# A two-layer SSD/conformer/short-convolution block on one core: opening reordered, last output pair computed stream by stream, C of the last layer for latent tokens only, output turned inside the last stage

## The reference

```
for i in range(DEPTH):
    last = i == DEPTH - 1
    mx = (silu(c) @ w_mod[i] + b_mod[i]) ...      # nine modulation rows, latent
    mc = (silu(c_ctx) @ w_mod[i] + b_mod[i]) ...  # the same, context
    x = swiglu_half(x, mx, 0, ...)
    ctx = swiglu_half(ctx, mc, 0, ...)
    uc = modulate(ctx, norm_pre[i, 1], mc[3], mc[4])
    if last:    # of the context only the final scan states are used
        xs, Bm, Cm, dt, A = ssd_inputs(uc @ w_in[i][:, :SSD_IN], ...)
        s_f = ssd_final_state(xs, dt[:, :, 0], A[0], Bm)
        s_b = ssd_final_state(flip_seq(xs), ..., flip_seq(Bm))
    else:
        yc, s_f, s_b = mixer(uc @ w_in[i], ...)
        ctx = gated_residual(ctx, yc @ w_out[i], ...)
        ctx = swiglu_half(ctx, mc, 2, ...)
    ux = modulate(x, norm_pre[i, 1], mx[3], mx[4])
    yx, _, _ = mixer(ux @ w_in[i], s_f, s_b, ...)
    x = gated_residual(x, yx @ w_out[i], ...)
    x = swiglu_half(x, mx, 2, ...)
```

## Time and profile before

| | us |
|---|---|
| median of 3 runs (2392.0 to 2395.12) | 2392.99 |
| the profiled execution | 2389.37 |
| its span, first to last instruction | 2387.3 |
| PE busy, share of the span | 94% |
| DVE, ACT, POOL busy | 52%, 41%, 9% |
| mean granted TensorE clock, share of full speed | 0.969 |

### The profile page before, as it was taken

One profiled execution on the slowest core, in us unless ns is written; L12 is line 12 of the kernel. 1 busy time (PEld: TensorE's weight loads), 2 busy tenths in 40 slices (PEclk: granted clock), 3 DMA queues, 4 the chain that ended last, 5 costly groups with the idle time before them and its releaser, 6 DMA issues. The chain is left out here.

```text
span 2387.3 us, 28755 instructions
## 1 busy us (share of the span) xinstructions
PE 2238.6 (94%) x11753; PEld 1902.1 (80%) x11753; DVE 1241.7 (52%) x1759; ACT 984.9 (41%) x1477; POOL 224.0 (9%) x139
## 2 busy tenths in 40 slices
PE   5999999998988989999999999999999988889998
PEld 5788888876676768788888778888888776779998
DVE  4544453347769743544444445333324578855554
ACT  5444443244465343434443343222323444454443
POOL 0000000023322300100000000000001332300000
PEclk8999999999999989899999998999998999989999
DMA  6455454312332213255454441323332233334553
GB/s 219 142 171 164 159 167 159 97 56 71 90 124 87 73 53 101 76 172 163 159 169 162 150 137 56 103 90 105 119 97 69 71 107 97 107 117 131 187 179 122
DMA packets 282544, 291.05 MB, mean 122 GB/s; under 512 B 8286, under 2 KB 275502, under 8 KB 282414
## 3 DMA queue, kind: packets, MB, share of 16 engines
q1 hardware_dynamic: 281619, 287.04, 37.4%
q10 hardware_dynamic: 795, 2.18, 0.3%
HBM read 288.02 MB, written 1.18 MB: 121 GB/s over the span
## 5 line engine op out<-in xcount | busy, mean ns | idle before, releaser
L85 ACT ACTIVATE split<-raw 128x1024 fp32r<-128x1024 f32 (+1 forms) x368 | 382.8, 1040 | 938.2 <-PE bank L133 927.6
L93 DVE TENSOR_TENSOR split<-raw,split 128x1024 fp32r<-128x1024 f32 (+1 forms) x304 | 364.8, 1200 | 715.3 <-ACT split L85 715.3
L131 PE MATMUL bank<-uh,split 128*128 128x512 f32 (+1 forms) x1344 | 488.6, 364 | 1.1 <-DVE split L93 1.1
L133 PE MATMUL bank<-uh,split 128*128 128x512 f32 (+1 forms) x1344 | 488.3, 363 | 0.0
L132 PE MATMUL bank<-ul,split 128*128 128x512 f32 (+1 forms) x1344 | 488.3, 363 | 0.0
L133 PEld LDWEIGHTS bank<-uh,split 128*128 128x128 f32 x1344 | 253.9, 189 | 40.2
L131 PEld LDWEIGHTS bank<-uh,split 128*128 128x128 f32 x1344 | 254.1, 189 | 38.6 <-issue 1.5
L132 PEld LDWEIGHTS bank<-ul,split 128*128 128x128 f32 x1344 | 254.1, 189 | 36.5
L131 PE MATMUL bank<-hh,split 128*128 128x512 f32 (+1 forms) x704 | 256.6, 364 | 0.9 <-DVE split L93 0.9
L131 PE MATMUL bank<-mix_uh,split 128*128 128x512 f32 (+1 forms) x608 | 231.9, 381 | 27.2 <-POOL split L100 16.4
L133 PE MATMUL bank<-hh,split 128*128 128x512 f32 (+1 forms) x704 | 255.7, 363 | 0.0
(11 more groups left out here) (225 smaller groups left out, 2974.8 us busy)
## 6 DMA issues: line engine op xcount, KB each, us to landing
raw_mod<-in_w_mod SPq DMA_DIRECT2D x64, 1024.0 KB, 4.8
raw<-in_ffn_w_gate SPq DMA_DIRECT2D x44, 1024.0 KB, 5.1
raw<-in_ffn_w_up SPq DMA_DIRECT2D x44, 1024.0 KB, 5.1
raw<-in_w_in SPq DMA_DIRECT2D x40, 1024.0 KB, 5.1
raw<-in_ffn_w_down SPq DMA_DIRECT2D x32, 1024.0 KB, 4.9
raw<-in_w_out SPq DMA_DIRECT2D x16, 1024.0 KB, 4.9
raw<-in_ffn_w_down SPq DMA_DIRECT2D x16, 768.0 KB, 4.3
decay<-cum_rows SPq DMA_DIRECT2D x48, 256.0 KB, 3.4
```

The source lines that it names most:

```text
L85: ins = K.nc.scalar.activation(K.wh[:, half, 0:kn, :], K.raw[:, slot, 0:kn, half * P:half * P + P], ACT.Copy)
L93: ins = K.nc.vector.tensor_tensor(K.wl[:, half, 0:kn, :], K.raw[:, slot, 0:kn, half * P:half * P + P], r32(K.wh[:, half, 0:kn, :]), ALU.su ...
L131: K.nc.tensor.matmul(bank[:, 0:tn], K.wh[:, half, k, :], h, start=first and k == 0, stop=False)
L133: ins = K.nc.tensor.matmul(bank[:, 0:tn], K.wl[:, half, k, :], h, start=False, stop=last and k == kn - 1)
```

## The change

In `OutProduct` the last pair of output tiles is computed for 256 tokens at a time: every part but the last for one stream and then the other, half by half; of the last part, both halves of stream 0, then both of stream 1. Sums, factor, residual, squares and second norm are made per stream, in two sets of signals, banks 5 and 4 for sums, 6 and 7 for factors. DVE adds squares in pairs, so that PE sums four tiles and not eight. The full tails have no warm-ups; the one at each stage's start has 4 for 8. The last pair takes its parts in the order 6, 8, 8. Four modulation halves move from feed-forward 0-2 to 1-0.

In the opening, `x` is loaded by ACT ahead of the parameters and turned after two modulation halves; DVE and ACT share the copies; the other halves run between squares, sums and parameters. Layer 1's parameters and the scan's small rows are loaded in feed-forward 0-0 (second trip) and turned there (trips 4 and 5). In mixer 1 the two C tiles (halves 14 and 15), their convolution and silu take latent tokens alone. The closing stage is gone: tiles are turned as they get ready, and stored as four transfers of 256 KB.

```diff
 def product_first_pair(K, pe, banks, uh, ul, tok):
     behind = 3
-    warm_pe(K, 8)
+    warm_pe(K, 4)
     pe.wait_ge(K.lo_done.sem, K.lo_done.at(2))
...
+        def part(half, i, nth, first, last, after_k=None):
+
+            s, a = self.streams[i]
+            if first:
+                pe.wait_ge(K.y_ready.sem, K.y_ready.at(3 + half + 2 * i))
+            k0, kn = self.kstart[part_no], self.parts[part_no]
+            closes = "half" if (s, a) == ends else "part" if last else None
+            product_half(K, pe, K.bank[2 - 2 * i + half], half, kn, lambda k: self.xh(k0 + k), lambda k: self.xl(k0 + k),
+                         (self.xtok[0] + a, CTX), first, last, nth, None, after_k, None, closes)
...
+                if pair < 3:
+                    if self.first[p] and pair >= 2:
...
+                elif not self.last[p]:
+                    for i in range(len(self.streams)):
+                        part(half, i, self.halves + n, self.first[p], False)
...
-                if self.mods and n == min(self.mods + 1, 2 * self.n_panels - 1):
+                if self.mods and n == self.mods + 1:
                     mod_turn_pe(K, pe, self.mod_group)
                 n += 1
-        warm_pe(K, 3)
-        pe.wait_ge(K.sq_added.sem, K.sq_added.at(7))
-        sums_pe(K, pe, K.sq[:, 0, :], self.tok, True, True)
-        warm_pe(K, 2)
-        rstd_pe(K, pe, self.tok, self.norms)
-        if self.norm_follows:
-            residual_rms_pe(K, pe, self.tok, self.y, self.norms + 1, self.norms - 1)
+        nth = self.halves + n - 2
+        for half in range(2):
+            part(half, 0, nth + half, False, True)
+        if len(self.streams) == 2:
+            def sums_after(k):
+                if k == 4:
+                    self.sums_pe(pe, 0)
+
+            def factors_after(k):
+                if k == 1:
+                    self.factors_pe(pe, 0)
+
+            part(0, 1, nth, False, True, sums_after)
+            part(1, 1, nth + 1, False, True, factors_after)
+            if self.mods:
+                pe.wait_ge(K.mod_evac.sem, K.mod_evac.own())
+            self.sums_pe(pe, 1)
+            self.factors_pe(pe, 1)
+            self.square_sums_pe(pe, 0)
+            self.factors_pe(pe, 0, 2)
+            self.square_sums_pe(pe, 1)
+            self.factors_pe(pe, 1, 2)
...
+        tile(0, 0)
+        tile(0, 1)
+        root(0, 1)
+        if len(self.streams) == 2:
+            tile(1, 0)
+            squares(0, 0, 1)
+            tile(1, 1)
+            squares(0, 1, 3)
+            root(1, 1)
+            squares(0, 3, 8)
+            squares(1, 0, 1)
+            root(0, 2)
+            squares(1, 1, 2)
+            split_ahead_act(K, act, (0,))
+            squares(1, 2, 5)
+            split_ahead_act(K, act, (1,))
+            squares(1, 5, 8)
+            root(1, 2)
+        elif self.norm_follows:
...
+        tile_squares(0, 0)
+        tile_squares(0, 1)
+        factors(0, 1)
+        if len(self.streams) == 2:
+            tile_squares(1, 0)
+            residual(0, 0, 5)
+            tile_squares(1, 1)
+            residual(0, 5, 7)
+            factors(1, 1)
+            residual(0, 7, 8)
+            for n in range(3):
+                pair(0, n)
+            residual(1, 0, 2)
+            pair(0, 3)
+            residual(1, 2, 6)
+            factors(0, 2)
+            pair(1, 0)
+            residual(1, 6, 7)
+            pair(1, 1)
+            residual(1, 7, 8)
+            split_ahead_dve(K, dve, (0,))
+            pair(1, 2)
+            pair(1, 3)
+            factors(1, 2)
+            split_ahead_dve(K, dve, (1,))
+        else:
+            residual(0, 0, 8)
...
+                if late and i == 1:
+                    late.sp(sp)
             next_panels(pairs - 1, out.src(0), out.src(1))
...
             for i in range(1, pairs):
                 trip(i, False)
+                if late and i == 4:
+                    late.pe(pe)
...
                 elif n > 1:
                     product_half(K, pe, K.bank[n % 2], n % 2, 8, lambda k: uh[:, k, :], lambda k: ul[:, k, :],
-                                 FULL if kind == "xbc" else part, True, True, n, None,
+                                 FULL if kind == "xbc" and not alone(last, tile) else part, True, True, n, None,
                                  scan_step if SCAN_AT <= n < Z_AT else None, plan.low_there(K, n))
...
+                    s0 = 1 if alone(last, t) else 0
+                    view = K.bank[6 + t % 2][:, :].rearrange("p (s n) -> p s n", s=2)[:, s0:]
...
+    def pe(self, pe):
+        K = self.K
+        pe.wait_ge(K.params_late.sem, K.params_late.at(16 * len(param_rows(K, 1))))
+        for n, rows in enumerate(PACK_ROWS):
+            ins = K.nc.tensor.transpose(K.bank[5 + n][:, 0:rows], self.pr[0:rows, n, :], K.ident[0:rows, 0:rows])
+        ins.then_inc(K.turn.inc(), 1)
+
...
-            for pack, row, src in param_rows(K, 0)[1::2]:
-                sp.dma_start(pr[row:row + src.shape[0], pack, :], src).then_inc(K.params_in.inc(16), 16)
...
-            for layer in range(1, L):
-                for pack, row, src in param_rows(K, layer):
-                    dst = pr[row:row + src.shape[0], layer * PACKS + pack, :]
-                    sp.dma_start(dst, src).then_inc(K.params_late.inc(16), 16)
-            for layer in range(L):
...
+            mods(0, 2)
             pe.wait_ge(K.x_in.sem, K.x_in.at(16 * TT))
             for j in range(8):
...
-            mod_turn_pe(K, pe, 0)
+            mods(2, 6)
+            for i in range(4):
+                pe.wait_ge(K.pair_ready[0].sem, K.pair_ready[0].at(i + 1))
+                sums_pe(K, pe, squares[:, 2 * i, :], FULL, 0, i == 0, i == 3)
+                mods(6 + i, 7 + i)
+            pe.wait_ge(K.res_ready.sem, K.res_ready.at(4))
+            pe.wait_ge(K.res_tail.sem, K.res_tail.at(4))
+            params(0)
+            mods(10, 12)
+            rstd_pe(K, pe, TOK, 1, 0, CTX)
+            mods(12, 16)
+            mod_turn_pe(K, pe, 0, 3)
...
+            mods(0, 2)
+            for j in range(1, 8, 2):
+                act.wait_ge(K.turn.sem, K.turn.at(2 + j))
+                nc.scalar.activation(K.res[:, j, :], K.bank[j % 4][:, :], ACT.Copy).then_inc(K.res_tail.inc(), 1)
+            mods(2, 6)
+            act.wait_ge(K.turn.sem, K.turn.at(9))
+            for j in range(8):
+                copied = (K.res_ready, K.res_tail)[j % 2]
+                act.wait_ge(copied.sem, copied.at(j // 2 + 1))
+                ins = nc.scalar.activation(squares[:, j, :], K.res[:, j, :], ACT.Square)
+                ins.then_inc(K.square_ready[0].inc(), 1)
+                if j % 2:
+                    mods(6 + j // 2, 7 + j // 2)
+            mods(10, 12)
             params(0)
-            mods(0)
-            for j in range(8):
-                act.wait_ge(K.turn.sem, K.turn.at(2 + PACKS + j))
-                nc.scalar.activation(K.res[:, j, :], K.bank[j % 4][:, :], ACT.Copy).then_inc(K.res_ready.inc(), 1)
-            next_rms_act(K, act, FULL, squares, 1)
-            for layer in range(1, L):
...
+            for j in range(0, 8, 2):
+                dve.wait_ge(K.turn.sem, K.turn.at(2 + j))
+                nc.vector.tensor_copy(K.res[:, j, :], K.bank[j % 4][:, :]).then_inc(K.res_ready.inc(), 1)
+            mods(2, 6)
+            for i in range(4):
+                pair_sums_dve(K, dve, squares, FULL, i, 0)
+                mods(6 + i, 7 + i)
+            mods(10, 14)
+            rstd_dve(K, dve, TOK, 1, 0)
+            mods(14, 16)
             mod_rows_dve(K, dve, 15, 0)
             split_ahead_dve(K, dve)
-            mod_out_dve(K, dve, 0, 0, 8, 0)
+            dve.wait_ge(K.turned.sem, K.turned.at(1 + PACKS))
...
+class Store:
...
+    def pe(self, pe):
+        K = self.K
+        for j in range(8):
+            done, n = (K.res_ready, POOL_TILES.index(j)) if j in POOL_TILES else (K.res_tail, OWN_TILES.index(j))
+            pe.wait_ge(done.sem, done.at(n + 1))
             for t in range(2):
...
...
+                bank = K.bank[self.BANKS[2 * (j // 4) + t]]
+                ins = K.nc.tensor.transpose(bank[:, j % 4 * P:j % 4 * P + P], K.res[:, j, CTX + t * P:CTX + t * P + P], K.ident[:, :])
+            ins.then_inc(K.turn.inc(), 1)
...
-            feed_forward(K, layer, 0, FULL, layer, 16 if layer == 0 else 68, layer == 0,
-                         12 if layer == 0 else 4, mixer_first(K, layer), (layer, 1))
+            feed_forward(K, layer, 0, FULL, layer, 16 if layer == 0 else 64, layer == 0,
+                         12 if layer == 0 else 8, mixer_first(K, layer), (layer, 1))
             mixer(K, layer, last, ff_first(layer, 1))
             after = ff_first(layer + 1, 0) if not last else []
             feed_forward(K, layer, 2, LATENT if last else FULL, None if last else layer + 1, 0, not last,
-                         0 if last else 24, after, None if last else (layer + 1, 0))
-        closing(K)
```

(37 more changed lines are left out.)

454 lines of the change are left out of this document (244 added, 210 removed).

## The result

The changed kernel takes 2365.23 us (median, 2361.32 to 2368.33), the kernel before 2392.49 beside it (2391.1 to 2395.12): ratio 0.988, interval 0.986 to 0.990. Forecast were 2360.3 and a range of 2350 to 2374. The gain is 27.3 us of the 32.7 worked out. The profiles differ by 21.0, and I read them stage by stage.

A forecast was written before the change was run, and what follows sets the result against it. PE was taken to bound the dense product stretches, with thin work in four tails, opening and closing. Terms 9.8 - 0.4 + 16.5 + 4.2 + 2.6 = 32.7 us gave a median of 2360.3, range 2350 to 2374.

The forecast's parts named there:

- opening: Before the first stage: modulation halves fill the norm's time, ACT carries it, start at 50.9 not 60.74; 9.8 us gained.
- late loads: Feed-forward 0-0: 18 small loads moved there fit on SP; three transposes and a wait cost PE 0.4 us.
- full tails: Four full output products: shorter stretches to the next stage, less dearer last pairs and sums inside; 16.5 us gained.
- C: Mixer 1: C tiles for latent tokens only, 48 matmuls shrink, half 15 waits 0.9 us for weights; 4.2 us gained.
- closing: End of the kernel: only the last two tiles remain when POOL and DVE end; 2.6 us gained.
- the walk behind the last product: Full tails: DVE leads, engines followed with each wait; next stage starts 14.9 us after the last product.
- the last pair with stream 0's sums inside: Full output products: two runs of 256 lose 8.3 us, stream 0's sums and factors inside products lose 4.4 us.
- Rival 1: Full tails late through handovers between DVE, ACT and PE, 3 us more each: 2372; chance 0.13.
- Four warm-ups fewer: 0: Stage starts: DVE's last low part, not PE, holds the first product pair, so dropping four warm-ups gains 0.
- Rival 2: Clock low after the tails, first product pairs 6.1 us late in each of four stages: 2385; chance 0.08.
- Rival 4: Slower: weight loads of 189 ns stop hiding behind 256-column streams, 66 us lost: 2426; chance 0.02.
- rival 3: Opening at half clock throughout: 2369; chance 0.09.

The follow-up runs named there:

- whole tails: Against the changed kernel, the four full output products and their tails put back as before, 512 tokens at a time with 13 warm-ups: 2381.65 us, ratio 0.995.
- warmed tails: Against the changed kernel, fifteen warm-ups put in each full tail between its sums: 2365.96 us.
- everything together: Against the changed kernel, opening factor behind the last modulation halves, late small loads from ACT's queue, and warm-ups in each full tail: 2367.79 us.
- both edits, the second time: Second run of the changed kernel with opening factor behind the last modulation halves and late small loads from ACT's queue: 2365.18 us.

## Why the prediction was right, and where not

The direction and the range hold, and the tails are the largest term, but two terms were too large. Terms in the order of the sum, forecast and measured in place (us):

| term | forecast | measured |
|---|---|---|
| opening | 9.8 | 5.6 |
| late loads | -0.4 | -1.4 |
| full tails | 16.5 | 12.5 |
| C | 4.2 | 4.1 |
| closing | 2.6 | 2.6 |
| sum | 32.7 | 23.4 |

The sum in place is 3.9 below the 27.3 of the medians, and that difference stays open. For the tails it counts the time from the first product of the last pair: 51.83, 42.90, 61.17 and 52.77 before, 208.7, against 192.2. Of these 16.5 us, 4.0 are not gained: four modulation halves moved out of that stretch of feed-forward 0-2 (three at 0.96 among the products, and the 1.1 behind them). Experiment and place agree on the rest, 11.9 and 12.5.

Stage by stage the two profiles differ by 5.6 (opening), 1.3, 1.0, 9.3, -0.1, 1.0 and 2.6 us, in all 20.7, the difference of the spans. The 9.3 of feed-forward 0-2 hold the 4.0 that moved to 1-0, and 3.3 from ahead of the last pair that no term has; there PE's longest wait for a modulation half's low part fell from 3.21 to 1.23 us, and why is not shown. The two mixers kept 1.0 and 1.0 us of the 2.8 (last pair and tail of mixer 0) and 4.1 (C) gained in them; their mean granted clock was 0.95 and 0.92 where it had been 0.96 and 0.94.

**Opening: the step that failed.** I let ACT carry it alone, ended the chain with its first split at 43.0, and took for granted that PE keeps up. The split ended at 47.71 (45.72 and 1.99). ACT had to wait for PE twice more than I counted: the last copy of x ended at 23.78, not at 20.8, and at 39.30 it had idled 1.89 us for PE's turning of the parameters. PE's first sixteen matmuls took 3.56 us from start to start and its turning of x 4.85, against 2.0 at 0.122 each and 3.66 in the kernel before, which makes 2.8 of the 3.0; the clock column reads 1.00 there (14.7 to 23.2), so why they are slow is not shown. The third error is the factor, which stands ahead of halves 12 to 15 in PE's queue: I did not ask what is queued behind its wait. Their matmuls began at 45.54, and moving the factor behind them is worth 2.2. The modulation rows were forecast for 46.2 and were there at 51.59: 3.0 for x, 1.9 for the parameters, 2.2 for the factor, less 1.6 that I had allowed too much between the last high part and the rows. Since I had put 1.1 on top of the chain (50.5 for 49.4), the start is 4.2 late and not 5.3. That the kernel with the factor last starts at 51.27, so near 50.9, is luck in part: x and the parameters are late there too, and the two allowances cover them. The parts of the gain were also misplaced: the order of the halves, as written, gave 2.4, the loads and copies 4.0.

**Late loads.** I had counted SP's issue time (nine us against thirteen of air) and not what the small transfers do to the queue. From 113 to 121 us SP issued eighteen; the gate panel behind them took 10.4 us to land, by the view of transfers from 110 to 135 us:

```profile
raw<-in_ffn_w_gate SPq DMA_DIRECT2D x1, 1024.0 KB, 10.4
```

The page's median for it is 5.2. ACT then waited 4.03 us for the modulation panel issued after it. In the other traces with these loads on SP the slip is 1.0 to 1.4 us.

**Tails: 4.0 too much.** The step that was mis-sized is the walk behind the last product. It is 16.05, not 14.9. Half clock costs 1.0 of it where my walk had 1.7, but at full clock the tail is 15.03 where the walk had 13.6. The remaining 1.4 lie in operations and hops between engines that I counted short, which were not separated. The other part came out right, the last pair with stream 0's sums inside at 12.7 in all, but by luck. In three stages it costs 2.62, 2.15 and 2.62: the sum and the factor inside products cost 0.4 to 0.5 us where I put 1.1. In feed-forward 0-2 the pair grew by 2.48 although three modulation halves left it, so it costs 5.4. There PE now waits longer for a modulation half's low part, before and after:

```profile
1393.34 1.22 PE L195 MATMUL bank<-mod_split,cond 128*128 128x256 f32 x8 [1.29 <-DVE mod_split L178]
```

```profile
1382.21 1.73 PE L197 MATMUL bank<-mod_split,cond 128*128 128x256 f32 x8 [2.48 <-DVE mod_split L180]
```

A likely cause is that the first part is now the short one, so that less product time covers that half's load and split; it was not tested alone. Behind the wait the granted clock is 0.75 for 6.8 us (1382.2 to 1389.0), where eight and 36 matmuls take 6.9 us for 5.4 at 0.122 each. The kernel with whole tails has the same order of parts and the same wait (2.71). Rival 1 (17.9 each) fell with the 16.05.

**Four warm-ups fewer: 0.** Against the kernel before that is so. But the new tail hands a lower clock to the latent stage, and with eight it would have lost 1.8 us there: the two edits belong together.

**Rival 2** (first pairs late) did not come in the changed kernel: 18.05 before, 18.05 after, in every full stage, at half clock for up to 6 us from the start. Its mechanism exists all the same. Where the low-clock stretch begins 4.9 to 5.2 us after the start, the pair ends at 18.83 (mixer 0 with warmed tails, feed-forward 0-2 with everything together) or 18.96 (feed-forward 0-0 with both edits, the second time): 0.8 to 0.9 us late, where the rival had 6.1. The Trainium skill ("TensorE: Matmul & The Clock Gate", section "Why this matters for your kernels") warns of idle gaps of PE between bursts of matmuls. In the tails, where the clock fell to 0.58 to 0.65, the trace agrees with the direction only: PE's longest idle time in the first tail is 1.25 us. **Rival 4** is refuted too: with weight loads at 189 ns as before, the last pair costs 32.70 for 30.08 us. That the opening runs at half clock throughout (rival 3) did not come either, but half of its price did, by another way.

**What stays open.** Small gains that the trace shows in their place (2.2 in the opening, 1.4 at the loads, 4 in warmed tails) did not reach the median, and three undone parts cost 3 to 4.5 us more than their place shows (C, tails, the halves' order). Low-clock stretches in the mixers go with the differences between traces. Why those stretches come where they come, and whether edits move them in one direction, no run here tells apart.

## What to carry to other kernels

When an instruction that waits moves, read its engine's queue behind it: here a factor that nothing read for nine more us held up four halves and 2.2 us of the opening. A batch of small loads costs the large load behind it more than its issue time. A stretch that shrinks may only have sent its work elsewhere: count the same instructions on both sides before the difference is called a gain. And a gain of 3 us can be checked here only in its place, by the trace: ten runs against nine tell means apart from some 4 us on. If the runs do not show it, say so.

## What was not expected of the hardware

Eighteen small loads (2 to 62 KB) on one queue doubled the time to landing of the 1024 KB panel behind them, 5.2 to 10.4 us; from a second queue and six at a time they did not.

The same program's runs differ by up to 15 us (2361.7 to 2376.4), and the mean granted clock goes with it (0.969 to 0.960). In mixer 0 a stretch of 88 us at a clock of 0.90 lies in the trace whose mixer took 6 us more, while PE was not busy throughout even at 1.00.

Keeping the clock at 1.00 in a tail took fifteen warm-ups (two records of 256 columns each); it saved 1.0 us in the tail and nothing at the end.
